# The second half of the sample's state parts of a head, issued in the next projection block

## The chip, the cores and the metric

The kernel runs on one core of one Trainium2 chip. The metric is the device time of one execution in microseconds (us). The kernel is written in Bass: every engine has an instruction stream of its own, written out by hand, and the streams meet at semaphores. The matrix products are in float32.

## The reference

The reference is one inference step of one decoder layer with three groups of heads: forgetting attention (FoX, 6 heads), HGRN2 (6 heads with a 128 x 128 state each) and memory cross-attention (4 heads). They share one input projection. A mixture of 32 experts follows. There are 256 prompt tokens and 8 x 4 sample tokens, so 288 tokens in all.

What matters here is HGRN2. Per head, with keys k, values v, queries q and decays f, the state obeys

```
S_t = diag(f_t) S_{t-1} + k_t v_t^T        o_t = S_t^T q_t
```

The prompt starts from a zero state and runs over 256 tokens; its last state is an output (`hgrn_state_p`). Each of the 8 sample sequences starts from its own given state (`state_hgrn`), runs over 4 tokens, and its last state is an output too (`hgrn_state_s`). The prompt is worked in 16 chunks of 16 tokens.

## The kernel before, in words

The 46 column blocks of the input projection, 128 columns each, are computed one after the other on TensorE. A block is 16 steps (`k` = 0 to 15) of a 128x128 weight against the 288 token columns, accumulated in one PSUM bank (`project`, line 1537); the profile has two matmul records for each step in float32. Inside `project` a function `between(k)` is called after step k, and other work of TensorE is slipped in there.

The last ten blocks, `last_block(n)` for n = 0 to 9, carry the state work of HGRN2. Block n = 1 to 6 works on head h = n - 1, and block n + 1 on what is left of it:

- after step 2, `keys_by_token(h)` (line 1610): three transposes of the keys; ScalarE copies them to `ktil` (lines 811 and 812).
- after step 6, `inter_prompt(h - 1)` (line 1645): 30 small products of the previous head's chunk states with its queries. Then `prompt_parts(h)` (line 1621): 8 products that give the 16 chunks' key-value parts in banks 2 to 5.
- after step 8, `inter_sample(h)` (line 1638): 8 products of the sample's given states with the queries.
- after steps 9 and 14, `sample_parts(h, 0)` and `sample_parts(h, 1)` (line 1630): one product each, of `ktil` with a masked copy of the values, `vmask[c]`, which gives the key-value parts of four of the eight sequences. Both halves use bank 6.

VectorE, per head, in this order: add the previous head's inter product to the outputs (line 1165); wait for `stp_out`, which says that the previous head's prompt state has been stored; wait for the prompt parts; one copy (line 1176) and 15 dependent steps (line 1178) that chain the 16 chunk states; scale the eight sample states by their decays (line 1184); add the first half of the sample's parts (line 1189), then the second half (line 1189 again), each raising `ds_used`; multiply the output gate (line 1191).

The first half waits for `ds_used` of the previous head's second half, and the second half for `ds_used` of its own head's first half, since all share bank 6:

```python
if h or c:
    pe.wait_ge(ds_used, 3 * h + c + (1 if c else 0))
pe.wait_ge(sm_set, 2 * h + c + 3)
```

GpSimd, per head, fills `vmask[0]` for head h when the previous head's first half has been computed, fills `vmask[1]` when its second half has (line 717 both; `ds_filled`), and then calls `states_out(h - 1)`: store the prompt's last state (line 702, 64 KB, raises `stp_out`), store the eight sample states (line 704, 512 KB), wait for that, and load the sample states of head h + 1 into the same buffer (line 707, 512 KB). ScalarE overwrites `ktil` of the sample only when the previous head's second half has been computed.

SyncE loads the projection's weights in slots. Two loads of 2 MB fall in this stretch. One is issued when block n = 2 has been computed (line 508), and one when n = 5 has (line 510), so they run beside the blocks of heads 2 and 5. Behind the ten blocks come the forget gate's columns (lines 1687 and 1691), the norms of heads, the prompt's attention, the sample's attention over the page cache, the output projection, routing, and the experts, whose weights are streamed.

Of the kernel before, what the change touches and what calls it, by code (L numbers as in the profile page):

```python
# [15 lines left out]
HF, HG, HM = 6, 6, 4  # L16
# [28 lines left out]
def build(nc, x_prompt, x_sample, cache_fox_k, cache_fox_v, cache_fox_logf, cache_mem_k, cache_mem_v,  # L45
# [29 lines left out]
    with ctx:  # L75
# [392 lines left out]
        def width(u):  # L468
            fox, h, qb = UNITS[u]
            return (qb + 1) * P if fox else MEM  # L470
# [1043 lines left out]
        def _(pe):  # L1514
# [20 lines left out]
            def project(bank, w, rhs, wt, c, m=P, between=None):  # L1535
                for k in range(KC):
                    last = pe.matmul(PS[0:m, bank, 0:w], wt[:, k, c:c + m], rhs[:, k, :], start=(k == 0), stop=(k == KC - 1))  # L1537
                    if between is not None and k < KC - 1:
                        between(k)
                last.then_inc(blk_filled, 1)  # L1540
# [56 lines left out]
            def values_by_token(f):  # L1597
                t, c, m = f // 2, (f % 2) * 4, 4 - 2 * (f % 2)
                t0, w = TILES[t]
                if f >= 2:  # L1600
                    pe.wait_ge(vt_drained, f - 1)
                for a in range(m):
                    last = pe.transpose(PS[0:w, 6 + f % 2, a * P:(a + 1) * P], raw[:, HI + c + a, t0:t0 + w], ident[:, :])
                last.then_inc(vt_filled, 1)

            def keys_by_token(h):
                if h:
                    pe.wait_ge(ds_used, 3 * (h - 1) + 1)
                for t, (t0, w) in enumerate(TILES):
                    last = pe.transpose(PS[0:w, 2, t * P:(t + 1) * P], raw[:, HFG + h, t0:t0 + w], ident[:, :])  # L1610
                last.then_inc(kt2_filled, 1)

            def prompt_parts(h):

                pe.wait_ge(kt2_drained, h + 1)
                if h == 0:
                    pe.wait_ge(vt_drained, 6)
                for t in range(2):
                    for r in range(4):
                        rows_r = slice(32 * r, 32 * r + 32)  # L1620
                        last = pe.matmul(PS[:, 2 + r, t * 2 * P:(t + 1) * 2 * P].rearrange("p (a v) -> p a v", a=2),
                                         ktil[rows_r, t, :], vpar[rows_r, :, t, h * P:(h + 1) * P], start=True, stop=True)
                last.then_inc(ds_filled, 1)

            def sample_parts(h, c):
# [4 lines that stand above are left out]
                pe.matmul(PS[:, 6, :], ktil[:, 2, :], vmask[c].rearrange("p b v -> p (b v)"), start=True, stop=True).then_inc(ds_filled, 1)  # L1630

            def inter_sample(h):
                pe.wait_ge(s_loaded[h % 2], 16 * (h // 2 + 1))
                if h:
                    pe.wait_ge(o_added, h)
                for b in range(NB):
                    c = SEQ + b * NL
                    last = pe.matmul(PS[:, 7, c:c + NL], s_in[h % 2][:, b, :], raw[:, HQ + h, c:c + NL], start=True, stop=True)
                last.then_inc(os_filled, 1)

            def inter_prompt(h):
                pe.wait_ge(ds_used, 3 * h + 1)
                for n in range(1, NCH):
                    for v in (slice(0, 64), slice(64, P)):
                        last = pe.matmul(PS[v, 7, n * CH:(n + 1) * CH], states[:, n - 1, v], raw[:, HQ + h, n * CH:(n + 1) * CH],
                                         start=True, stop=True)
                last.then_inc(oi_filled, 1)

            def last_block(n):
                def between(k):  # L1650
                    if n == 0 and 2 <= k < 14 and k % 2 == 0:
                        if k == 2:
                            pe.wait_ge(hg_done, 4)
                        values_by_token(k // 2 - 1)
                    h = n - 1
                    if k == 2 and 0 <= h < HG:
                        keys_by_token(h)
                    if k == 6:
                        if 0 < h <= HG:
                            inter_prompt(h - 1)  # L1660
                        if 0 <= h < HG:
                            prompt_parts(h)
                    if 0 <= h < HG:
                        if k == 8:
                            inter_sample(h)
                        if k in (9, 14):
                            sample_parts(h, k // 14)
                if n < 2:
                    pe.wait_ge(blk_drained, 44)
                else:  # L1670
                    pe.wait_ge(blk_drained, 44 + n - 1)
                if n in (0, 3):
                    pe.wait_ge(w_in_slot[1 - n // 3], 96 + 48 - 16 * (1 - n // 3))
                    slot = 1 - n // 3
                if n in (6, 8):
                    slot = (8 - n) // 2
                    pe.wait_ge(w_in_slot[slot], 144 + 16 * (1 - slot))
                slot, c = [(1, n), (0, n - 3), (1, n - 6), (0, n - 8)][(n >= 3) + (n >= 6) + (n >= 8)]
                project(n % 2, T, xT, wslot[slot], c * P, between=between)

            for n in range(10):
                last_block(n)
            pe.wait_ge(wff_in, 32)
            for j in range(4):
                for i in range(4):
                    k = 4 * i + j
# [56 lines left out]
            for s in range(NU + 2):  # L1743
                if s < NU:
                    fox, h, qb = UNITS[s]
# [4 lines left out]
                    k = raw[:, FK + h, 0:width(s)] if fox else mraw[:, h, :]  # L1750
# [13 lines left out]
                if s >= 2:  # L1764
                    u = s - 2
                    fox, h, qb = UNITS[u]
# [328 lines left out]
```

## Time and profile before

| what | us |
| --- | --- |
| median of 3 executions | 2030.17 |
| lowest and highest of the 3 | 2029.45, 2033.73 |
| the profiled execution, its own time | 2027.35 |
| span of the profiled execution | 2025.8 |
| granted TensorE clock over that span, share of full speed | 0.874 |
| TensorE matmul busy | 1605.6 (79%) |
| VectorE busy | 439.1 (22%) |
| ScalarE busy | 239.0 (12%) |
| GpSimd busy | 77.4 (4%) |

The profiled execution is a fourth one, apart from the three. Its span is the time between its first and last instruction; 1.55 us lie around it. PE is TensorE's matmuls, PEld its weight loads (they can overlap matmuls), DVE VectorE, ACT ScalarE, POOL GpSimd, SP SyncE; a q behind an engine's name is its sequencer, which issues transfers. A matmul's end is modelled in the trace, so its distance from start to next start is the safer measure. "Idle before" a row, in square brackets, is the engine's idle time ahead of it and who ended it.

### The profile page before, as it was taken

How to read it: one execution, taken by the hardware profiler on the slowest of the kernel's cores; microseconds unless marked ns; L12 is line 12 of the kernel's file. 1: busy time of each engine (PE TensorE's matmuls, PEld its weight loads, DVE VectorE, ACT ScalarE, POOL GpSimd, SP SyncE). 2: the span in 40 equal slices, each digit the busy share in tenths (PEclk: the TensorE clock that was granted, in tenths of full speed). 3: DMA queues.
4: the chain of work that ended last, by engine and by line, in shares of the span. 5: the costliest groups of instructions: out<-in, count | busy, mean ns of one | idle time of the engine just before them, and what ended most of it. 6: DMA issues, size and time to landing. Idle time of an engine off the chain costs nothing.

```text
span 2025.8 us, 25494 instructions
## 1 busy us (share of the span) xinstructions
PE 1605.6 (79%) x10013; PEld 955.9 (47%) x10013; DVE 439.1 (22%) x1206; ACT 239.0 (12%) x534; POOL 77.4 (4%) x140
## 2 busy tenths in 40 slices
PE   5999999989999888899966767667676766757656
PEld 4777777766656555567741323223132321413213
DVE  2100166645134333201130110102001010200103
ACT  3000110110133233311130000000000000000000
POOL 1000000022000022200000000000000000000000
PEclk9999999999976999999977877869687877878878
DMA  6443332223113688763539999999999999999995
GB/s 220 155 147 132 125 125 92 94 91 120 48 53 113 214 296 302 272 205 110 208 130 403 421 421 421 421 422 422 422 422 422 422 422 422 422 422 422 421 421 228
DMA packets 141090, 559.68 MB, mean 276 GB/s; under 512 B 16707, under 2 KB 72068, under 8 KB 90180
## 3 DMA queue, kind: packets, MB, share of 16 engines
q1 hardware_dynamic: 132756, 522.55, 65.3%
q0 software_dynamic: 8272, 36.25, 5.3%
q8 instruction: 45, 0.74, 0.1%
q14 instruction: 17, 0.14, 0.0%
HBM read 547.68 MB, written 11.08 MB: 276 GB/s over the span
## 4 chain that ended last, share of the span: by engine, by line
PE 50%; DMA 36%; DVE 5%; issue 3%; ACT 2%; SPq 2%; POOL 0%; POOLq 0%; DVEq 0%; ACTq 0%
PE PS L1537 18%; DMA arena<-in_w_up_e_dram 17%; DMA arena<-in_w_down_e_dram 10%; DMA arena<-in_w_gate_e_dram 8%; PE PS L1954 7%; PE PS L1903 6%; PE PS L1984 2%; SPq L575 2%; PE PS L1842 2%; PE PS L1791 2%; DVE arena L1178 1%; PE PS L1938 1%; PE PS L1578 1%; PE PS L1813 1%; DMA arena<-in_cache_mem_v_dram 1%
## 5 line engine op out<-in xcount | busy, mean ns | idle before, releaser
L1954 PE MATMUL PS<-arena 128*32 128x512 f32 x2048 | 352.0, 851 | 222.7 <-DMA arena<-in_w_up_e_dram 125.5
L1537 PE MATMUL PS<-arena 128*128 128x288 f32 (+1 forms) x1728 | 433.7, 406 | 3.8 <-DVE arena L1021 1.5
L1537 PEld LDWEIGHTS PS<-arena 128*128 128x128 f32 x1728 | 327.6, 192 | 96.0 <-issue 13.1
L1954 PEld LDWEIGHTS PS<-arena 128*32 128x32 f32 x2048 | 79.8, 148 | 489.4 <-issue 217.3
L1984 PE MATMUL PS<-arena 128*32 128x512 f32 x1024 | 144.5, 721 | 81.5 <-DMA arena<-in_w_down_e_dram 81.5
L1903 PE MATMUL PS<-arena 128*128 128x288 f32 x512 | 129.8, 413 | 0.4 <-DVE arena L1291 0.4
L1446 DVE TENSOR_TENSOR arena<-arena,PS 128x512 f32<-128x512 f32 x8 | 5.5, 688 | 552.0 <-PE PS L1954 552.0
L1984 PEld LDWEIGHTS PS<-arena 128*32 128x32 f32 x1024 | 35.9, 129 | 184.0 <-DMA arena<-in_w_down_e_dram 95.0
L1903 PEld LDWEIGHTS PS<-arena 128*128 128x128 f32 x512 | 97.1, 192 | 32.1 <-issue 5.5
L1938 PEld LDWEIGHTS PS<-arena 128*128 128x128 f32 x768 | 89.6, 197 | 8.3 <-issue 6.8
L1938 PE MATMUL PS<-arena 128*128 128x128 f32 x768 | 91.8, 281 | 1.4 <-DVE arena L1420 1.4
L1791 PE MATMUL PS<-ident,arena 128*128 128x128 f32 x384 | 52.8, 293 | 18.6 <-ACT arena L886 14.2
L2001 PE MATMUL PS<-arena 128*128 128x288 f32 x256 | 64.2, 409 | 0.0
L1454 DVE TENSOR_TENSOR arena<-arena,PS 128x288 f32<-128x288 f32 x128 | 58.2, 454 | 3.7
L1451 DVE COPY arena<-PS 128x512 f32<-128x512 f32 x16 | 11.1, 692 | 216.2 <-PE PS L1984 216.2
L1791 PEld LDWEIGHTS PS<-ident,arena 128*128 128x128 f32 x384 | 46.3, 151 | 24.5 <-ACT arena L886 16.1
L2001 PEld LDWEIGHTS PS<-arena 128*128 128x128 f32 x256 | 48.0, 190 | 19.3 <-ACT arena L969 5.9
L964 ACT ACTIVATE arena<-PS 128x512 f32<-128x512 f32 x8 | 4.8, 597 | 363.6 <-PE PS L1971 363.6
L736 POOL DMA_DIRECT2D arena<-in_cache_fox_v_dram x64 | 34.7, 543 | 255.0 <-issue 129.7
L1842 PE MATMUL PS<-arena 128*32 128x128 f32 x768 | 32.6, 284 | 13.5 <-DVE arena L1283 7.2
L1092 DVE SCALAR_TENSOR_TENSOR arena<-arena 128x576 f32<-128x576 f32 x3 | 2.3, 758 | 186.6 <-ACT arena L785 186.6
L962 ACT ACTIVATE arena<-PS 128x512 f32<-128x512 f32 x8 | 4.8, 597 | 317.2 <-PE PS L1954 317.2
(334 smaller groups left out, 1290.2 us busy)
## 6 DMA issues: line engine op xcount, KB each, us to landing
arena<-in_w_gate_e_dram SPq DMA_DIRECT2D x128, 1024.0 KB, 18.8
arena<-in_w_up_e_dram SPq DMA_DIRECT2D x128, 1024.0 KB, 19.7
arena<-in_w_down_e_dram SPq DMA_DIRECT2D x128, 1024.0 KB, 17.9
arena<-in_w_in_dram SPq DMA_DIRECT2D x14, 3072.0 KB, 10.8
arena<-in_cache_fox_k_dram SPq DMA_DIRECT2D x64, 384.0 KB, 6.6
arena<-in_cache_fox_v_dram POOLq DMA_DIRECT2D x64, 384.0 KB, 4.2
arena<-in_w_out_dram SPq DMA_DIRECT2D x8, 2048.0 KB, 8.6
arena<-in_w_mem_kv_dram SPq DMA_DIRECT2D x2, 3072.0 KB, 17.5
```

Source lines behind the costliest of these rows:

```text
L575: sp.dma_start(unit[slot].rearrange("p (k n) -> p k n", n=src.shape[4]), src[ds(p * XQ + x, 1), g % 4].rearrange("e p k n -> p (e k) n")). ...
L736: pool.dma_start(vpages[:, g, :], v_pages[ds(page, 1)].rearrange("g t n -> t (g n)")).then_inc(v_loaded, 16)
L1178: ins = dve.scalar_tensor_tensor(out=states[:, n, :], in0=states[:, n - 1, :], scalar=decays[:, h, n:n + 1], in1=delta(n), op0=ALU.mult, o ...
L1454: dve.tensor_tensor(yT[:, n, :], yT[:, n, :], PS[:, 2 + n % 4, 0:T], ALU.add).then_inc(part_added, 1)
L1537: last = pe.matmul(PS[0:m, bank, 0:w], wt[:, k, c:c + m], rhs[:, k, :], start=(k == 0), stop=(k == KC - 1))
L1791: last = pe.transpose(PS[:, bank + h // 4, (h % 4) * P:(h % 4 + 1) * P], kpage[g][:, h * P:(h + 1) * P], ident[:, :])
L1842: pe.matmul(o, dprobT[:, g, 32 * i:32 * i + 32], vpages[:, g, h * P:(h + 1) * P], start=(g == 0), stop=False)
L1903: last = pe.matmul(PS[:, n % 2, 0:T], wo_slot[(n // 2) % 3][:, k, c:c + P], cat[:, k, :], start=(k == 0), stop=(k == KC - 1))
L1938: last = pe.matmul(o, h_scaled[:, t, c * P:(c + 1) * P], pick_tok[:, t, :, :].rearrange("p x s -> p (x s)"), start=(t == 0), stop=(t == 2))
L1954: last = pe.matmul(PS[x * SLOTS:(x + 1) * SLOTS, which, :], xgT[:, kk, x * SLOTS:(x + 1) * SLOTS], wt[:, k, :], start=(kk == 0), stop=(kk ...
L1984: last = pe.matmul(PS[x * SLOTS:(x + 1) * SLOTS, YB[n], :], hT[:, q, x * SLOTS:(x + 1) * SLOTS], wt[:, n * 512:(n + 1) * 512], start=(q == ...
L2001: last = pe.matmul(PS[:, 2 + n % 4, 0:T], yslot[:, n * P:(n + 1) * P], gate_slot[:, :], start=True, stop=True)
```

## The change

For every head, `sample_parts(h, 1)` is called after step 1 of the block that follows the head's own, instead of after step 14 of its own. Its arguments, waits and operands are the same; `sample_parts(h, 0)` stays after step 9.

```diff
                     if 0 <= h < HG:
                         if k == 8:
                             inter_sample(h)
-                        if k in (9, 14):
-                            sample_parts(h, k // 14)
+                        if k == 9:
+                            sample_parts(h, 0)
+                    if 0 < h <= HG and k == 1:
+                        sample_parts(h - 1, 1)
```

TensorE's order before, from the first half of head 0 to the block of head 1. L1630 is `sample_parts`, L1537 a step of the projection, L1610 the keys' transposes:

```order
L1630 MATMUL PS<-arena,ktil 128x512 [waits sm_set]
L1537 MATMUL PS<-arena 128x288 x5
L1630 MATMUL PS<-arena,ktil 128x512 [waits sm_set,ds_used]
L1537 MATMUL PS<-arena 128x288
L1537 MATMUL PS<-arena 128x288 [waits blk_drained]
L1537 MATMUL PS<-arena 128x288 x2
L1610 MATMUL PS<-ident,arena 128x128 [waits ds_used]
```

And TensorE's order at the same place with the change:

```order
L1630 MATMUL PS<-arena,ktil 128x512 [waits sm_set]
L1537 MATMUL PS<-arena 128x288 x6
L1537 MATMUL PS<-arena 128x288 [waits blk_drained]
L1537 MATMUL PS<-arena 128x288
L1630 MATMUL PS<-arena,ktil 128x512 [waits sm_set,ds_used]
L1537 MATMUL PS<-arena 128x288
L1610 MATMUL PS<-ident,arena 128x128 [waits ds_used]
```

The second product stands eight projection steps behind the first instead of five, and one step ahead of the keys' transposes of the next head instead of four. The streams of the other engines are the same, instruction by instruction.

## Rows read from the trace of the kernel before

**Rows 1.** The page, part 4: the chain that ended last, shares by engine.

```profile
PE 50%; DMA 36%; DVE 5%; issue 3%; ACT 2%; SPq 2%; POOL 0%; POOLq 0%; DVEq 0%; ACTq 0%
```

**Rows 2.** Waits, 420 to 524 us: waiter, releaser, us in total, times, longest.

```profile
PEld PS L1630 <- DVE arena L1189: 10.9, 6, 1.8
...
PE PS L1630 <- DVE arena L1189: 8.2, 6, 1.4
```

**Rows 3.** The chain in order of time, 516 to 524 us: start, us, what.

```profile
518.09 3.88 PE PS L1537 x16
```

**Rows 4.** Timeline of TensorE, block of head 1: start us, us, engine, line, operation.

```profile
436.14 2.10 PE L1537 MATMUL PS<-arena 128*128 128x288 f32 x8
438.08 0.49 PE L1610 MATMUL PS<-ident,arena 128*128 128x128 f32 x3
...
442.31 1.15 PE L1621 MATMUL PS<-arena,ktil 32*128 32x256 f32 x16
...
446.73 1.02 PE L1630 MATMUL PS<-arena,ktil 128*128 128x512 f32 x2
447.59 2.59 PE L1537 MATMUL PS<-arena 128*128 128x288 f32 x10
451.54 1.12 PE L1630 MATMUL PS<-arena,ktil 128*128 128x512 f32 x2 [1.36 <-DVE arena L1189]
452.50 2.10 PE L1537 MATMUL PS<-arena 128*128 128x288 f32 x8
```

**Rows 5.** Timeline of VectorE, the same block.

```profile
442.42 0.44 DVE L1165 TENSOR_TENSOR arena<-arena,PS 128x272 f32<-128x272 f32 x1 [4.68 <-PE PS L1645]
443.59 0.29 DVE L1176 COPY arena<-PS 128x128 f32<-128x128 f32 x1 [0.73 <-PE PS L1621]
443.91 5.71 DVE L1178 SCALAR_TENSOR_TENSOR arena<-arena,decays,PS 128x128 f32<-128x128 f32 x15
449.54 1.22 DVE L1184 TENSOR_TENSOR arena<-arena,decays 128x1024 f32<-128x1024 f32 x1
450.80 0.69 DVE L1189 TENSOR_TENSOR arena<-arena,PS 128x512 f32<-128x512 f32 x1
...
453.31 0.79 DVE L1191 TENSOR_TENSOR arena<-arena,sq 128x288 f32<-128x288 f32 x1
```

**Rows 6.** Timeline of GpSimd, block of head 2.

```profile
453.73 0.61 POOL L702 DMA_DIRECT2D out_dram<-arena  x1
454.33 0.90 POOL L704 DMA_DIRECT2D out_dram<-arena  x1
461.64 0.89 POOL L707 DMA_DIRECT2D arena<-in_state_hgrn_dram  x1 [6.41 <-DMA out_dram<-arena]
```

**Rows 7.** Landings: line 702 all six and the fifth, 704 all and second, 707, 510.

```profile
DMA to landing us min/median/max: 1.8/1.9/5.2
...
DMA to landing us min/median/max: 5.0/5.0/5.0
...
DMA to landing us min/median/max: 3.8/3.8/8.2
...
DMA to landing us min/median/max: 7.0/7.0/7.0
...
DMA to landing us min/median/max: 4.6/4.7/4.8
...
DMA to landing us min/median/max: 11.1/11.1/11.1
```

**Rows 8.** Stretches: length, busy of PE, PEld, DVE, ACT, POOL, PEclk, DMA share, GB/s.

```profile
420.00:524.00 104.00, 95.81 (x812) 72.02 (x811) 54.35 (x126) 8.70 (x27) 25.61 (x30) 1.00 0.32 96
...
590.00:600.00 10.00, 8.20 (x36) 5.58 (x37) 1.42 (x5) 3.79 (x8) 0.00 (x0) 0.50 0.00 0
600.00:610.00 10.00, 8.87 (x56) 5.54 (x56) 0.00 (x0) 2.40 (x3) 0.00 (x0) 0.94 0.82 283
```

## The prediction

> **What bounds the kernel now.** I read the page first: the chain that ended last is half TensorE and a third transfers [rows 1]. The reader is to see that no one engine bounds the whole run; each stage has its own bound. The change touches one stage alone, the ten last projection blocks, of which seven carry the state work of the six HGRN heads, from 420 to 524 us. So I read the waits of that stretch next. There TensorE waited six times, once per head, on VectorE line 1189, 1.36 us each and 8.2 us together, and every one of these waits is in front of the second multiplication of `sample_parts`, line 1630; its weight load stood for 1.8 us each [rows 2]. Otherwise TensorE has no idle time to speak of in the stretch: 95.8 of 104 us are busy, and 95.8 + 8.2 fills it [rows 8]. It is thus the engine that sets the pace there, and its six waits are on the path.
>
> Why it waits is in the two timelines, TensorE's and VectorE's, of the block of head 1 [rows 4, 5]. The prompt parts start at 442.31. VectorE then makes a copy and a chain of 15 steps for the prompt's states (443.59 to 449.5), scales the sample's eight states (449.54) and adds the first half (450.80). Only then is the one PSUM bank of the sample's parts free, at 451.54. TensorE has in that time the sample's inter product, the first half (446.73) and five steps of the projection from 447.59. A step is 3.88/8 = 0.485 us from start to start, two records each [rows 3], so it would have been free at 447.59 + 5 x 0.485 = 450.02.
>
> **The change, part by part.** It adds, removes and resizes nothing. Six multiplications with their weight loads go three projection steps later on TensorE: past step 15 of their own block and steps 0 and 1 of the next. The order of VectorE, ScalarE, GpSimd and SyncE stays.
>
> *Wait removed.* Now the half starts at 451.54 where it could start at 450.02: 1.52 us. It also costs 0.96 us from start to next start (451.54 to 452.50), since its weight load stands exposed, where the first half costs 0.86 (446.73 to 447.59) [rows 4]. So 1.52 + 0.10 = 1.62 us a head is the most that can go, 9.7 us over six.
>
> *Wait left over.* VectorE frees the bank 451.54 - 442.31 = 9.23 us after the prompt parts start. TensorE gets to the new place 5.28 us (442.31 to 447.59) plus eight steps (10 to 15, then 0 and 1) of 0.485, 9.16 us after the same start. Nothing of that VectorE chain is shortened, so the two arrive almost together: 0.07 us is waited, and I leave the 0.10 us of the exposed weight load. Gain per head 1.62 - 0.17 = 1.45 us, **8.7 us for six**. That is a tie, with no slack: whatever makes VectorE's chain start late now reaches TensorE in full.
>
> *What is queued behind the moved work.* On VectorE the second addition and the gate's product (0.69 and 0.79 us) move from the head of the block into its steps 2 to 5. The next thing that it does there, line 1165, came only at 442.42, 5.8 us into the block [rows 5]; that gap covers them, and I cost them at nothing. On ScalarE the copy of the keys waits for the half as well, but the keys' transposes (438.08, behind step 2) still come after it [rows 4]: nothing.
>
> *GpSimd's queue.* This is the edit's cost. GpSimd fills the second mask when the half is done, and behind that, in its program's order, stores the previous head's prompt state (line 702), which VectorE waits for ahead of its next chain (`stp_out`), then stores and reloads the sample states (lines 704 and 707). From the half's start to line 702's issue take 453.73 - 451.54 = 2.19 us [rows 4, 6]. I count from step 0 of a block (436.14 + 0.485 = 436.63 for head 1's, 452.99 for head 2's). The half now starts at 0.97 + 0.07 = 1.04 in it, so the store is issued at 3.23 instead of 0.74. VectorE wants to begin its chain at 443.59 - 436.63 = 6.96 today, and at 6.96 + 1.03 = 7.99 with the half in front of it. The store lands after 1.9 us at the median [rows 7], and the waiting engine moves some 0.3 us after a landing (454.33 + 7.0 against 461.64) [rows 6, 7]: 5.4, covered with 2.6 us to spare. In two blocks of the seven a load of 2 MB of projection weights starts with the block and takes 11 us, and there the store takes 5.2 and 5.0 us [rows 7]. That gives 3.23 + 5.2 + 0.3 = 8.73 and 8.53, later than 7.99 by 0.74 and 0.54. As there is no slack left, **1.3 us is paid back**. This is the unknown price, as no row shows this store issued in the middle of such a load. Its ends are nothing (1.9 us, the quiet row) and 11.1 us, the whole load's. I take 5.2 and 5.0, the same store beside the same load, 0.55 us behind its start.
>
> By the Trainium skill ("DMA: Bandwidth & Descriptors", Queues, rings and completion order) each DMA engine alternates between the rows of queues that have work, packet by packet. By that rule the store would not wait for the load's end wherever it is issued, and the sum stays at 1.3 us; were the rule not to hold here, it would be the 13.3 us of the first rival.
>
> *Reload of the sample states.* Line 704 follows 0.60 us behind 702, at 3.83, lands after at most 8.2 and line 707 after 4.8 more: 3.83 + 8.2 + 0.3 + 4.8 = 17.1 us [rows 6, 7]. It is read in the next block, behind that block's prompt parts, which start 5.68 us in: 14.7 + 5.7 = 20.4. Covered by 3 us.
>
> *Sum.* 8.7 - 1.3 = 7.4 us less. What follows the stretch has no start of its own: the loads on SyncE's and GpSimd's queues are issued behind semaphores that these blocks raise, so I let the whole rest move up. Against the profiled execution's own 2027.35 us that is 2020.0; that execution is 2.8 us below the median of the three others, 2030.17, so the forecast for the median is **2022.8 us**.
>
> **The rivals.**
>
> *The store queues behind the weights (slower).* If the prompt state's store, issued 3.2 us into the block, is held until the 2 MB load ends, it takes 11.1 us instead of 5.2: 3.23 + 11.1 + 0.3 = 14.63, which is 6.64 us late, in two blocks: 13.3 us against the 8.7, so 4.6 slower, 2034.8 us. It decides from a landing of 8.8 us on (4.35 us late twice). Against it: even the 512 KB store landed after at most 8.2 us beside the load [rows 7]. A landing of 8.2 us costs 3.7 twice and leaves 1.2 us of gain: 2029.0.
>
> *The clock further on.* In this stretch the granted clock is 1.00, the 2.4 GHz level, with the waits in it, so the removed waits buy no clock. Later it is not steady: TensorE ran at 0.50 (1.2 GHz) from 590 to 600 us, at 0.94 from 600 to 610 [rows 8]. A start earlier by 7 us may put other work under either level. If the 8.87 us busy of the second stretch ran at the level of the first, it would take 8.87 x 0.94/0.50 = 16.7, 7.8 more; if the 8.20 us of the first ran at the second's, 3.8 less. So 2019.0 to 2030.6. For it: the executions before spread over 4.3 us. Against: that spread is the same kernel's, and a median takes most of it out. The Trainium skill ("TensorE: Matmul & The Clock Gate", What's actually happening) says that the number of slow matmuls of one kernel varies between runs with where they fall against the gate's own windows. By that rule this rival is luck in each execution rather than an effect of the change; this trace, one execution, can't tell.
>
> *The wait only moves.* If the tie falls the wrong way by more than 0.07 us, for instance as VectorE's steps run later beside a TensorE that doesn't pause, the half waits at its new place. To eat the gain it would need 1.4 us a head; the chain's rows hold nothing that could grow so. About 2030.
>
> *Swallowed behind.* The last stage is set by transfers [rows 1]. If one of its loads were not tied to this stretch, the gain would end there: 2030.2. Against it: every issue stands behind a semaphore.
>
> **How the numbers follow.** Forecast 0.66: 2020.5 (9.7 us, no wait and no late store) to 2024.5. Clock helping 0.10; clock against 0.08, mostly within 0.2% of before; store at about 8 us 0.05, within; store behind the load 0.04, slower; swallowed 0.04 and wait only moved 0.03, within. About 0.2%, 4 us, is what a measurement of this kernel can tell from no change. So faster by more than that 0.66 + 0.10 = 0.76, within 0.08 + 0.05 + 0.04 + 0.03 = 0.20, slower 0.04. The range goes from 2018.0, where most of the helping clock is in, to 2028.0, which takes half of the clock against; outside are the other half (0.04) and the 0.16 of the last four cases.
>
> **What would show it.** In the profile after, the wait of line 1630 on VectorE's line 1189 falls from 8.2 us to under 1 us; blocks of the heads come every 14.9 us instead of 16.36; the start of the chain's copy, line 1176, waits for a store in the blocks of heads 2 and 5 alone, by under 1 us each, and TensorE for VectorE as long in the block behind. Wrong, if line 702 takes over 6 us to land in those blocks, if the half still waits a microsecond per head, or if the stretch is 7 us shorter and the total isn't.

## The result, and the profile after

| what | before, us | changed, us |
| --- | --- | --- |
| first comparison, median of 6 each | 2028.40 | 2016.08 |
| lowest and highest | 2022.04, 2033.73 | 2013.88, 2017.06 |
| profiled execution, its own time | 2027.35 | 2015.53 |
| its span | 2025.8 | 2013.9 |
| its granted clock | 0.874 | 0.879 |

The ratio is 0.9945, with a 95% interval of 0.9933 to 0.9958: faster, as forecast, by 8.5 to 13.6 us instead of 7.4, and the median lies 1.9 us under the range given. Over four comparisons (below) the means of the two kernels differ by 7.9 us, but the single comparisons gave from 6.2 to 12.4.

The waits of the ten blocks after, 418 to 524 us (waiter, releaser, us in total, times, longest):

```profile
DVE arena L1176 <- DMA out_dram<-arena: 2.1, 2, 1.1
...
PE PS L1630 <- DVE arena L1189: 0.5, 2, 0.3
```

These answer to [rows 2]: TensorE's 8.2 us at line 1630 have become 0.5, in two blocks of the six, and a wait that was not there has come, VectorE's for the prompt state's store, also in two blocks.

TensorE's timeline after, heads 0 to 3:

```profile
430.61 1.02 PE L1630 MATMUL PS<-arena,ktil 128*128 128x512 f32 x2
431.47 4.04 PE L1537 MATMUL PS<-arena 128*128 128x288 f32 x16
435.42 1.12 PE L1630 MATMUL PS<-arena,ktil 128*128 128x512 f32 x2
436.38 0.65 PE L1537 MATMUL PS<-arena 128*128 128x288 f32 x2
...
446.37 4.04 PE L1537 MATMUL PS<-arena 128*128 128x288 f32 x16
450.32 1.13 PE L1630 MATMUL PS<-arena,ktil 128*128 128x512 f32 x2
...
461.27 4.04 PE L1537 MATMUL PS<-arena 128*128 128x288 f32 x16
465.52 1.12 PE L1630 MATMUL PS<-arena,ktil 128*128 128x512 f32 x2 [0.20 <-DVE arena L1189]
```

Against [rows 4]: the moved half comes every 14.90 us (435.42, 450.32) instead of 16.36. Eight steps from 431.47 would end at 435.35; the half starts at 435.42 and takes 0.96 to the next start. So 0.07 us of waiting and 0.10 of exposed weight load are left, the tie as it was worked out. That the load is exposed shows in the timeline of the weight loads, where the half's load begins together with its product, at 435.42:

```profile
435.42 0.30 PEld L1630 LDWEIGHTS PS<-arena,ktil 128*128 128x128 f32 x2 [0.37 <-DVE arena L1189]
```

The first half's load begins at 430.37, 0.24 us ahead of its product. The block of head 2 is longer, 465.52 - 450.32 = 15.20. Why, VectorE's and GpSimd's timelines of that block say:

```profile
457.57 0.29 DVE L1176 COPY arena<-PS 128x128 f32<-128x128 f32 x1 [1.02 <-DMA out_dram<-arena]
```

```profile
452.52 0.60 POOL L702 DMA_DIRECT2D out_dram<-arena  x1
453.11 0.90 POOL L704 DMA_DIRECT2D out_dram<-arena  x1
460.75 0.89 POOL L707 DMA_DIRECT2D arena<-in_state_hgrn_dram  x1 [6.74 <-DMA out_dram<-arena]
```

The store is issued 3.24 us into the block (step 0 starts at 446.37 + 6 x 0.485 = 449.28), lands after 5.0 us at 457.5, and VectorE starts its chain at once. Of its 1.02 us of idle time 0.73 are there in every block, before and after, so the store makes the chain 0.3 us late. In the chain of waits of the block of head 5 it stands as a link of its own, the landing took 5.1 us there:

```profile
497.52 5.08 DMA out_dram<-arena
...
502.62 0.30 DVE arena L1176
```

TensorE is now busy all through the stretch, where [rows 8] had 95.81 of 104 us:

```profile
420.00:524.00 104.00, 103.54 (x845) 78.35 (x844) 54.68 (x127) 9.35 (x28) 25.59 (x30) 1.00 0.32 96
```

The stretch from the first keys' transpose (line 1610) to the forget gate's first product (line 1687 before, 1689 after) took 543.84 - 423.58 = 120.26 us before and 535.99 - 423.82 = 112.17 after: **8.1 us less**. The spans differ by 11.9. The other 4 us are behind the stretch, which took 1482.0 us to the end before and 1477.9 after, with the same instructions. Most of it lies in three stages: the output projection, from its first product to the gather's (lines 1905 and 1940 of the changed kernel), took 169.4 us before and 167.7 after, the gather from there to the experts' first product (line 1956) 16.5 and 15.8, and what follows to the end 966.7 and 965.6. Before, 10 us where the output projection has begun:

```profile
874.00:884.00 10.00, 10.00 (x36) 7.58 (x35) 0.00 (x0) 0.41 (x1) 0.00 (x0) 0.83 1.05 339
```

After, 8 us earlier:

```profile
866.00:876.00 10.00, 10.00 (x43) 7.85 (x42) 0.00 (x0) 0.41 (x1) 0.00 (x0) 1.00 1.07 343
```

The column to read is the third from the end, the granted clock, 0.83 against 1.00, and the count of matmul records in brackets, 36 against 43 in a fully busy 10 us. In the gather and the experts' first products the clock was 0.78 and 0.83 before (1044 to 1054 and 1054 to 1064 us) against 0.96 and 1.00 after (8 us earlier each). This was an effect of the change or the luck of two executions; the first comparison can't say which, and the experiments went to that.

### The profile page after: what moved, and what is told of

Its sections match the earlier page's. It is cut to its first block, busy times and chain, and to the rows that moved or that the text cites. A ratio compares the mean times of both kernels' runs of the same rounds, so it can differ in the third digit from the quotient of the medians.

```text
span 2013.9 us, 25494 instructions
## 1 busy us (share of the span) xinstructions
PE 1594.0 (79%) x10013; PEld 952.8 (47%) x10013; DVE 439.5 (22%) x1206; ACT 238.9 (12%) x534; POOL 77.2 (4%) x140
## 4 chain that ended last, share of the span: by engine, by line
PE 51%; DMA 37%; DVE 4%; issue 3%; ACT 2%; SPq 2%; POOL 0%; POOLq 0%; DVEq 0%; ACTq 0%
PE PS L1537 19%; DMA arena<-in_w_up_e_dram 17%; DMA arena<-in_w_down_e_dram 10%; DMA arena<-in_w_gate_e_dram 8%; PE PS L1905 6%; PE PS L1956 6%; PE PS L1986 3%; SPq L575 2%; PE PS L1844 2%; PE PS L1793 2%; PE PS L1578 1%; PE PS L1940 1%; PE PS L1815 1%; DMA arena<-in_cache_mem_v_dram 1%; PE PS L1713 1%
## 5 line engine op out<-in xcount | busy, mean ns | idle before, releaser
L1956 PE MATMUL PS<-arena 128*32 128x512 f32 x2048 | 338.5, 822 | 228.1 <-DMA arena<-in_w_up_e_dram 130.9
L1537 PE MATMUL PS<-arena 128*128 128x288 f32 (+1 forms) x1728 | 434.2, 407 | 3.4 <-DVE arena L1021 1.1
L1537 PEld LDWEIGHTS PS<-arena 128*128 128x128 f32 x1728 | 327.7, 192 | 95.7 <-issue 12.9
L1986 PE MATMUL PS<-arena 128*32 128x512 f32 x1024 | 148.5, 738 | 84.3 <-DMA arena<-in_w_down_e_dram 84.3
```

The lines of the kernel that those rows point to most:

```text
L1956: last = pe.matmul(PS[x * SLOTS:(x + 1) * SLOTS, which, :], xgT[:, kk, x * SLOTS:(x + 1) * SLOTS], wt[:, k, :], start=(kk == 0), stop=(kk ...
L1986: last = pe.matmul(PS[x * SLOTS:(x + 1) * SLOTS, YB[n], :], hT[:, q, x * SLOTS:(x + 1) * SLOTS], wt[:, n * 512:(n + 1) * 512], start=(q == ...
```

## The experiments

Twelve runs of nine kernels were made in three jobs, each on a chip of its own. "Stretch" is from the first keys' transpose to the forget gate's first product; "rest" is from there to the end of the span.

**The two kernels again.** No edit.

> The kernel before, unchanged, profiled and timed once more, to see how much one kernel's time varies and where. Theory 'local' (the change shortens only the ten blocks, by some 8 us; the other 3 to 4 us between the two traces are luck of the granted clock in single executions): another profile of the same kernel has its clock-dependent places (the output projection's start, the gather, the first experts) as good as the changed kernel's in some executions, and the times spread over 5 us or more, 2022 to 2034. Theory 'phase' (the clock that is granted downstream depends on how far into the program the work stands, the same in each execution): the new profile has the low clock at the same places as the first one of this kernel, 0.83 at the output projection's start and 0.78 and 0.83 in the two 10 us stretches of the gather.

> The changed kernel, unchanged, profiled and timed once more. Stretch from the first keys' transpose (line 1610) to the forget gate's first product (line 1689): 112.2 us again, within 0.1, against 120.3 before. 'Local': the ratio over these rounds is 0.996 (8.1 us of 2028) with the clock evened out; 'phase': 0.9945 or less again, 11 to 12 us, and the profile shows 1.00 at the output projection's start and 0.96 and 1.00 in the gather, as in the first profile of it.

> The changed kernel a third time. So far its ratio to the kernel before was 0.9945 (6 executions each) and 0.9972 (11 against 34), two intervals that just do not meet. If the change is worth the 8.1 us of its stretch and the rest is the granted clock's luck, this one lies between them or beside them, around 0.996; if the first comparison was right it is 0.9945, if the second, 0.997. The stretch from line 1610 to 1689 is 111.8 to 112.2 us again.

> The changed kernel once more, as the zero of a series of delays behind the ten blocks. Over 23 executions so far its mean is 2018.25 against 2027.0 of 65 of the kernel before, 8.8 less. 'Local': 8 to 9 us under before again, ratio 0.996. 'Phase': 11 us or more, 0.9945.

| | executions | mean, us | median, us | ratio to before, 95% | stretch | rest |
| --- | --- | --- | --- | --- | --- | --- |
| before, first profile | | | | | 120.26 | 1482.0 |
| b_again | 12 | 2027.15 | 2027.24 | 1.0004 (0.9992, 1.0015) | 120.24 | 1484.1 |
| changed, first | 6 | 2015.88 | 2016.08 | 0.9945 (0.9933, 0.9958) | 112.17 | 1477.9 |
| a_again | 11 | 2020.05 | 2021.02 | 0.9972 (0.9961, 0.9982) | 111.79 | 1477.2 |
| a_third | 6 | 2017.33 | 2016.63 | 0.9949 (0.9931, 0.9967) | 112.06 | 1478.3 |
| a_fourth | 12 | 2020.11 | 2020.19 | 0.9972 (0.9960, 0.9984) | 112.39 | 1482.6 |

The stretch repeats, 120.25 before and 112.1 in the mean of four after; 111.79 is further off than the 0.1 us that a_again's expectation allowed. What varies in it is the store: it landed after 4.76 and 4.96 us in a_again and after 5.25 and 5.08 in a_fourth, and no other head's block changed.

The whole does not repeat: the changed kernel ran between 2013.88 and 2024.35 us in 35 executions, the kernel before between 2021.45 and 2035.12 in 100. The means are 2018.9 and 2026.8, 7.9 us apart, with a 95% interval of 6.7 to 9.1 from the spread of the single times. The stretch's 8.1 lies in it. But by comparison the means differ by 12.4, 6.3, 11.4 and 6.2 us, with standard errors of 1.7, 0.9, 1.5 and 1.0, so they fall into two pairs, further apart than the spread of single executions makes likely. The ratio of 0.996 that 'local' gave was met by none of the four: the first comparison and a_third lie near the 0.9945 of 'phase', and a_again and a_fourth, with 0.9972, above both. What differs from job to job stays open.

The rest of the profiled executions varies as well, from 1477.2 to 1484.1 without a change in it. Between two profiles of the changed kernel, a_again and a_fourth, 4.5 us lie between the forget gate and the output projection alone:

```profile
535.47:864.39 328.92, 279.35 (x2601) 179.17 (x2600) 102.79 (x312) 110.12 (x251) 40.25 (x72) 0.88 0.56 194
```

```profile
535.79:869.17 333.38, 284.34 (x2601) 184.59 (x2600) 102.97 (x312) 110.11 (x251) 40.27 (x72) 0.86 0.55 192
```

The work is the same, and the granted clock is 0.88 against 0.86. It is so in all fourteen profiles: this part took 332.8 to 335.5 us in the eight with 0.86 and 328.8 to 332.4 in the six with 0.87 or 0.88. At the start of the output projection the second profile of before did not have the low clock that the first had (167.7 us for that stage instead of 169.4). So the low clock there was not a fixed property of the kernel before.

**Does the place in time set the clock behind?** Unused products behind the ten blocks of the changed kernel, 8, 16 and 24:

```diff
             for n in range(10):
                 last_block(n)
+            for k in range(16):
+                pe.matmul(PS[:, 4, 0:T], wslot[0][:, 0, 0:P], xT[:, k % KC, :], start=True, stop=True)
```

> The changed kernel with 16 projection-sized products, unused, behind the ten blocks: 16 x 0.485 = 7.8 us, so that all that follows starts where it did before the change. 'Local': 2016 + 7.8 = 2024, that is some 3 to 4 us below the kernel before in the first comparison or 0.3 us below it once the clock's luck is evened out. 'Phase': all of the gain is gone, clock places as in the profile of before, 2027 to 2028, ratio 1.000 within 0.0005.

> Changed kernel with 8 unused products behind the ten blocks, 8 x 0.485 = 3.9 us (3.85 by the first series). 'Local' (the clock behind the blocks is luck of each execution, no function of where the work stands): mean is that of the changed kernel in this job + 3.9, within 2 us. 'Phase' (it depends on the position): off that line by 3 us or more, up or down.

> 16 unused products again, 7.8 us. The first time its mean was 9.3 us above the changed kernel on the same chip and 3 us above the kernel before, where 7.8 and -0.3 were expected. 'Local': this time 7.8 within 2 us, ratio to before 1.000 within 0.001. 'Phase': 9 to 11 us above the changed kernel again, ratio 1.0014 or more.

> 24 unused products, 11.7 us. 'Local': mean of the changed kernel + 11.7 within 2 us, ratio to before 1.0018. 'Phase': off that line by 3 us or more.

| | added by trace, us | mean, us | over the changed kernel of its job | ratio to before, 95% |
| --- | --- | --- | --- | --- |
| delay8 | 3.9 | 2022.87 | 2.8 | 0.9990 (0.9972, 1.0009) |
| delay16 | 7.7 | 2029.34 | 9.3 | 1.0014 (1.0000, 1.0028) |
| delay16_again | 7.7 | 2029.24 | 9.1 | 1.0016 (1.0003, 1.0029) |
| delay24 | 11.7 | 2030.60 | 10.5 | 1.0019 (1.0010, 1.0029) |

"Added by trace" is the stretch less the 112.1 of the changed kernel. The means lie -1.1, +1.6, +1.4 and -1.2 us from the line (the changed kernel of the job and what was added), all within the 2 us that 'local' allowed in the last three runs, while 'phase' wanted 3 or more in delay8 and delay24. Their standard errors are 1.1 to 1.3 us, and 2.0 in delay8, where one execution took 2004.17 us, 15 below its next; its median is 2024.59, 4.4 above the changed kernel's.

The two runs of delay16 speak against 'local' all the same. All that follows starts there as late as before the change (stretch 119.8 against 120.25), and the whole should have taken as long as before or 0.3 us less. It took 3.3 and 2.9 us more, with standard errors of 1.1 and 0.9. The first run fits neither expectation. The second is what 'phase' had said of it, 9 to 11 us above the changed kernel and a ratio of 1.0014 or more, and outside the 0.001 that 'local' allowed the ratio. But 'phase' as first stated, where the same place gives the same time, is missed too, as 1.0014 is not 1.000 within 0.0005. In the profiles the output projection took 168.5 and 168.7 us in the two, 169.4 in delay24 and in the first profile of before, and 167.7 to 167.8 in the ten others, with the second profile of before among them. So the clock behind the stretch varies from execution to execution, and it is not shown that this is all: a dependence of 1 to 3 us on the place in time, or on the unused products themselves, stays possible.

**The tie.** The half one step earlier:

```diff
-                    if 0 < h <= HG and k == 1:
+                    if 0 < h <= HG and k == 0:
```

> The changed kernel with the second half behind step 0 of the next block instead of step 1. My tie: VectorE frees the bank 9.23 us after the prompt parts' start, TensorE would be there after 9.16 - 0.49 = 8.67, so each head waits 0.56 us, 0.49 more than at step 1: heads' blocks every 15.39 us instead of 14.90, the stretch from line 1610 to 1689 is 6 x 0.49 = 2.9 us longer in all, 115.1; in the two blocks with the late store less is added (the chain starts 0.49 later anyway, the store is issued at the same distance), 2.5 to 2.9 us in all. Rival (the wait at the old place had another cause than VectorE's chain): the stretch stays at 112.2.

```profile
435.44 1.13 PE L1630 MATMUL PS<-arena,ktil 128*128 128x512 f32 x2 [0.39 <-DVE arena L1189]
...
450.83 1.12 PE L1630 MATMUL PS<-arena,ktil 128*128 128x512 f32 x2 [0.39 <-DVE arena L1189]
```

That is TensorE's timeline of it: the half every 450.83 - 435.44 = 15.39 us, to the hundredth what was expected, with a wait in every head. The stretch was 114.44, 2.3 us over the changed kernel's, a little less than the 2.5 to 2.9 expected. In the two blocks with a weights' load VectorE does not wait for the store here at all, so there only 0.49 - 0.30 is lost: 4 x 0.49 + 2 x 0.19 = 2.3. VectorE's chain is what TensorE waited for; the rival falls.

And one step later than the change, ahead of the keys' transposes:

```diff
-                    if 0 < h <= HG and k == 1:
-                        sample_parts(h - 1, 1)
+                    if 0 < h <= HG and k == 2:
+                        sample_parts(h - 1, 1)
                     if k == 2 and 0 <= h < HG:
                         keys_by_token(h)
```

> The second half behind step 2 of the next block, just ahead of the keys' transposes, one step later than the change has it. The bank is then free 0.4 us before TensorE comes in the blocks with no late store, so the exposed weight load (0.10) and the 0.07 of waiting go: 0.17 us less in four heads, blocks every 14.74 us. GpSimd's store of the prompt state is issued 0.4 us later, VectorE waits longer for it in the blocks of heads 2 and 5, and TensorE's wait behind these stays about where it is (0.2 to 0.5 each). The stretch from line 1610 to 1689: 111.3 to 111.7 us. Rival (the tie costs nothing that can be had back): 112.0 to 112.2.

Stretch 111.36, as expected: no wait in four heads. In the blocks of heads 2 and 5 the store is issued later still, and VectorE waits 1.6 us for it instead of 1.1. From the timelines of VectorE and of TensorE:

```profile
455.97 0.29 DVE L1176 COPY arena<-PS 128x128 f32<-128x128 f32 x1 [1.55 <-DMA out_dram<-arena]
```

```profile
463.92 1.12 PE L1630 MATMUL PS<-arena,ktil 128*128 128x512 f32 x2 [0.25 <-DVE arena L1189]
```

**The store.** GpSimd issues the prompt state's store ahead of the second mask, so that it stands behind nothing the change has moved:

```diff
                     if h:
+                        if c:
+                            prompt_state_out(h - 1)
                         pool.wait_ge(ds_filled, 3 * (h - 1) + 2 + c)
```

> The changed kernel, and GpSimd stores the previous head's prompt state ahead of filling the second mask, so the store no longer waits for the moved half. VectorE's line 1176 no longer waits for a transfer in any block (2.1 and 1.7 us before), TensorE's 0.5 us of idle time at line 1630 goes with it: stretch 111.5 to 111.7 us instead of 111.8 to 112.2. Rival (the late store is only a symptom, the load of weights slows VectorE or TensorE itself in these two blocks): TensorE still waits 0.2 us in the blocks of heads 2 and 5.

Stretch 111.54, 0.6 under the changed kernel, and VectorE waits for no transfer. GpSimd's timeline, where line 701 is the store (the edit shifts the line numbers):

```profile
448.42 0.60 POOL L701 DMA_DIRECT2D out_dram<-arena  x1 [1.06 <-DVE arena L1183]
```

It goes out at 448.42, before the block of head 2 and its load of weights begin, and lands after 1.9 us. The halves now come every 14.90 us in all the blocks. The late store was the cause of the two long blocks.

**Both edits.** Line 1635 is `sample_parts` here.

> Both: behind step 2, and the store first. No wait of TensorE at line 1630 and no exposed weight load in any head: the bound of 9.7 us under the kernel before is reached, stretch 120.26 - 9.7 = 110.6 us, blocks every 14.74 us. Total 1.2 to 1.6 us under the changed kernel, which the times cannot tell apart by themselves; ratio to before 0.9955 if the clock's luck evens out.

```profile
436.52 1.02 PE L1635 MATMUL PS<-arena,ktil 128*128 128x512 f32 x2
...
451.24 1.02 PE L1635 MATMUL PS<-arena,ktil 128*128 128x512 f32 x2
...
465.97 1.02 PE L1635 MATMUL PS<-arena,ktil 128*128 128x512 f32 x2
```

The half's record is 1.02 us in every head like the first half's, and comes every 14.72 and 14.73 us. The stretch is 110.46, 9.8 us under before: the bound is reached. Its mean of 6 executions is 2016.73 beside 2017.33 of the changed kernel on the same chip, a difference that the times can't show, and not the 1.2 to 1.6 us expected. The ratios of this job were 0.9947 (0.9929, 0.9966) for step2, 0.9944 (0.9923, 0.9965) for store_first and 0.9944 (0.9924, 0.9963) for both; step0 had 0.9975 (0.9958, 0.9991) in its own.

## Why the prediction was right or wrong

**Right: the place, the cause, the tie.** The wait of 1.36 us a head was VectorE's chain. Removed are 1.62 us a head, and 0.17 are left in a head with no late store: period 16.36 - 1.45 = 14.91 forecast, 14.90 measured. Moving the half by one step either way confirmed it from both sides (15.39 us a head one step earlier, 14.73 one later).

**Right: the price on GpSimd's queue, at half its size.** The store was issued at 3.24 us in the block (3.23 forecast), VectorE waited for it in the blocks of heads 2 and 5 alone (1.02 and 1.08 us, 0.73 of which it waits in every block), and the landings took 5.0 and 5.1 us, so the first rival, which needed 8.8, is out. But 0.74 + 0.54 = 1.3 us was the term, and the half came late by 0.30 (465.52 against 461.27 + 3.88 + 0.07) and 0.35: 0.65 us. The mis-sized step is the 0.3 us from a landing to the waiting engine, which I took from GpSimd's line 707. VectorE went on 0.05 us after it (452.52 + 5.0 to 457.57). With that, the sum is 9.72 - 6 x 0.17 - 0.65 = 8.05 us, and the stretch gave 8.09 in the first pair of profiles.

**Right, as far as it can be told: nothing swallowed.** The gain of the stretch is 8.1 us and the means of the whole differ by 7.9; as single comparisons gave 6.2 to 12.4, a loss of a microsecond or two behind the stretch would not have shown.

**Wrong: the range, by the step that set the clock rival aside.** The step that failed put all that lies behind the stretch at no change, for I wrote that the spread of 4.3 us "is the same kernel's, and a median takes most of it out". Three executions did not show the spread: it is 14 us over 100. And medians don't take it out: those of before were 2028.4, 2025.8, 2028.0 and 2026.1 in the four comparisons, those of the changed kernel 2016.1, 2021.0, 2016.6 and 2020.2. The forecast of 2022.8 missed the first median by 6.7 us, in three parts. The median that it starts from, 2030.17, is 3.4 above the mean of before. The gain was 0.5 more than 7.4 by the means. And the first median of the changed kernel lies 2.8 below its own mean, 2018.9, which would have been in the range. So it is in part luck that the number fell outside. A range around one median of this kernel needs some 5 us to either side for the spread alone, by these medians, before any unknown of the change.

**Right in kind, weighed too low: the clock further on.** This rival was priced from two pieces of 10 us out of 1482, at 3.8 us of help at most. The traces have 4.5 us between two profiles of one kernel in a single part of the rest, with a granted clock of 0.88 against 0.86. Of the 4 us behind the stretch in the first pair of profiles most are in stages where the granted clock differs. That they are luck of single executions, as that rival had it at the last, is likely and not shown: the two runs of delay16 lie 3 us over the kernel before with the same start of the rest, and the four comparisons fall into two pairs.

## What to carry to other kernels

When a wait of an in-order engine is removed by moving the waiting instruction back, work out when the releaser is done against when the engine gets to the new place; here the margin was under a tenth of a microsecond, and one step more with the store put first gave the rest. Follow what is queued behind the moved instruction's semaphore on every other queue: a mask held back a 64 KB store, and the store held VectorE. And judge a change of 0.4% on the stretch that it touches, anchor to anchor in two traces (112.1 against 120.25, each within 0.3 us), since the whole-program median moved by 5 us between comparisons of identical kernels. Such a figure says what the change did in its stretch; what it does to the clock behind, it can't say.

## What the runs showed of the hardware

A product whose semaphore wait is not yet met when TensorE reaches it costs 0.10 us more from start to start than its twin (0.96 against 0.86), even when the wait itself is only 0.07: its weight load begins with the product (435.42), where the twin's begins 0.24 us ahead. A 64 KB store on GpSimd's queue lands in 1.9 us alone and in 4.8 to 5.3 beside SyncE's 2 MB load, whether it is issued 0.5 or 3 us behind that load's start. The load itself landed after 10.9 to 11.2 us with the stores of 64 and 512 KB issued 0.5 us behind it, as in both profiles of before, and after 8.1 to 8.7 with the 512 KB store, alone or with the other, 3 us or more behind it, as in all twelve others. After a landing VectorE went on within 0.05 us, GpSimd after some 0.3. The same kernel's time varied over 10 to 14 us from execution to execution.
